# The sample tile's turn behind the first token tile, and a layer norm in parts of 160 and 384 tokens

## The chip, the cores and the metric

The program runs on one core of a Trainium2 chip. The metric is the device time of one execution in microseconds. Before the change it is 1164.78 us, the median of three runs from 1162.54 to 1170.73.

## The reference, cut to what matters

A two-layer decoder trunk is run on 512 prompt tokens and on 32 sample tokens (8 sequences of 4), all in float32, width 1024. Layer 0 mixes tokens with a short convolution and a windowed attention, layer 1 with a Conformer convolution module. Each is followed by a mixture of experts (32 experts, two for each token). What the change touches is the middle of layer 1:

```
def odd_mixer(h, w_pw1, b_pw1, dw_w, dw_b, ln_g, ln_b, w_pw2, b_pw2, conv_buf):
    ...
    c = causal_dwconv(u_ext, dw_w) + dw_b
    c = jax.nn.silu(layer_norm(c, ln_g, ln_b))
    return c @ w_pw2 + b_pw2, u_ext[:, -(C_KERNEL - 1):]
...
        x = x + y
        x = x + hier_moe(rms_norm(x, p['g_ffn'][layer]), ...)
```

The layer norm runs over the 1024 channels of each token. The 1024 x 1024 product behind it is followed by a residual add, an RMS norm and a router (36 logits for each token).

## The kernel before

The 544 tokens lie in five tiles: tiles 0 to 3 hold 128 prompt tokens each, tile 4 the 32 sample tokens. The convolution's output `cT` has channels in the partitions (8 blocks of 128) and tokens along the rows, so the layer norm's sums over channels are matmuls with a matrix of 1/1024.

`LN_PART` cuts the tokens into two parts, which pass through the layer norm one behind the other. Before the change the first part is tokens 256 to 543 (288 columns: tiles 2, 3 and the sample tile), the second tokens 0 to 255 (256 columns: tiles 0 and 1). I call them part A and part B. The steps are:

- DVE subtracts the mean from part A and then from part B, 8 instructions each (L1735).
- ACT squares part A (L1078), POOL squares part B (L826).
- PE sums the squares of A (`variance(0)`, L2359), keeps busy with five matmuls without use (L1796), multiplies the samples' rows with the weights (`project_samples`, L2038), sums the squares of B (`variance(1)`, L2359).
- For each part: ACT takes the root (L1081), DVE its reciprocal (L1739) and scales 8 blocks (L1747), ACT applies silu to them (L1085). ACT has a table to load between root and silu, 1.28 us each time.

Then come the tiles, in the order `ODD_ORDER` (4, 2, 3, 0, 1), on PE in `project`. A tile of 128 tokens is 16 matmuls (L2081), 8 for each half of the output's columns; the trace shows each float32 matmul as two records. For the sample tile `project_samples` does this already. The rest of a tile's work is: ACT moves the samples' sums out of PSUM (L854, the sample tile only), DVE adds bias and residual to X (L1155, L1162), PE turns the tile by eight transposes (`turn`, L1788) into PSUM banks 6 and 7, DVE copies it to SBUF (`keep`, L1168), PE multiplies by the router's weights (`router`, L2101), DVE makes logits and picks experts (`logits`, `pick_...`). A tile's turn stands between the two halves of the next tile's matmuls, its router in the middle of the second half. The sample tile's turn must also wait until the variance of part B has been read from bank 7 (`std_ready`).

The order on each engine is the order in which the code is written; each engine waits at semaphores. `experts(1)` follows: it ranks the tokens by expert, gathers their rows, and runs 32 experts, whose weights come in over the SP queue into six slots (L540, L542 ahead, L599 and L603 as slots come free). A token's rank in its expert goes by tile order (`ODD_ORDER`), in both layers. Tokens beyond an expert's first 64 are worked on in further jobs.

Of the kernel before, what the change touches and what calls it, by code (L numbers as in the profile page):

```python
# [35 lines left out]
TOK = SEQ + SAMPLES  # L36
# [19 lines left out]
PE_CONV = (1, 4, 6, 7)  # L56
DVE_CONV = tuple(c for c in range(KD) if c not in PE_CONV)
PW1_SLOT = (2, 3, 0, 1)
LN_PART = ((256, TOK), (0, 256))
ODD_ORDER = (4, 2, 3, 0, 1)  # L60
PART_AT = (2, 5, 7)
DVE_TAPS = (((0, 1, 17),), ((0, 17, 31),), ((2, 1, 25),), ((2, 25, 31), (3, 1, 10)), ((3, 10, 25),),
            ((3, 25, 31), (5, 1, 19)), ((5, 19, 31),), ())
# [75 lines left out]
def program(nc, x_in, w_mix0, kv_in, w_out, w_pw1, w_pw2, w_moe, smalls, consts, masks, rows, st_a, st_c,  # L139
            y_out, k_out, v_out, ua_p_out, ua_s_out, uc_p_out, uc_s_out):  # L140
    ctx = ExitStack()
    with ctx:
# [272 lines left out]
        def tiles_of(call):  # L415


            return list(enumerate(ODD_ORDER if call % 2 else range(TILES)))

# [675 lines left out]
        def _(dve):  # L1095
# [48 lines left out]
            def norm_and_route(call, done):  # L1144

                n = call // 2
                logits, pick_group, pick_first, pick_second, places = routing(n)

                def update(s, h):
                    i = ODD_ORDER[s]  # L1150
                    r = ROWS[i]
                    cols = slice(512 * h, 512 * h + 512)
                    if call == 3 and h == 0:

                        link(nc.vector.tensor_tensor(X[0:r, i, :], X[0:r, i, :], brow[0:r, :], ALU.add))  # L1155
                    if s == 0:
                        dve.wait_ge(spread_kept, n + 1)
                        src = xn_of(call, s, i)[0:r, cols]
                    else:
                        dve.wait_ge(done, 2 * s + h)  # L1160
                        src = psum[0:r, 2 * (s % 2) + h, :]
                    nc.vector.tensor_tensor(X[0:r, i, cols], X[0:r, i, cols], src, ALU.add).then_inc(x_half, 1)  # L1162

                def keep_half(s, h):
                    i = ODD_ORDER[s]
                    r = ROWS[i]
                    dve.wait_ge(turned, 10 * call + 2 * s + h + 1)
                    nc.vector.tensor_copy(  # L1168
                        turned_tile(s)[:, 4 * h:4 * h + 4, 0:r],
                        psum[:, 6 + h, :].rearrange("p (k t) -> p k t", k=4)[:, :, 0:r]).then_inc(hT_ready, 1)  # L1170

                def keep(s):
                    keep_half(s, 0)
                    keep_half(s, 1)

                def inverse(s):
                    i = ODD_ORDER[s]
                    r = ROWS[i]
                    dve.wait_ge(root_ready, TILES * call + s + 1)
                    nc.vector.reciprocal(stat[0:r, 2, i:i + 1], stat[0:r, 1, i:i + 1]).then_inc(inv_ready, 1)  # L1180

                last = TILES - 1
                update(0, 0)
                update(0, 1)
                for s in range(1, TILES):
                    update(s, 0)
                    keep(s - 1)
                    inverse(s - 1)
                    logits(s - 1)
                    if s == last:  # L1190
                        keep_half(last, 0)
                        pick_group(s - 1)
                    update(s, 1)
                    if s < last:
                        pick_group(s - 1)
                        pick_first(s - 1)
                        pick_second(s - 1)
                pick_first(last - 1)
                keep_half(last, 1)
                inverse(last)  # L1200
                pick_second(last - 1)
                logits(last)
                pick_group(last)
                pick_first(last)
                pick_second(last)
                places()
# [548 lines left out]
            update = combine(1)  # L1755
# [13 lines left out]
        def _(pe):  # L1769
# [292 lines left out]
            def project(call, src, blocks, weights, done, after_first=None):  # L2062
# [3 lines left out]
                for s, i in tiles_of(call):  # L2066
                    r, b = ROWS[i], 2 * (s % 2)
                    if s >= 2:
                        pe.wait_ge(x_half, 10 * n + 2 * (s - 2) + 2)
                    if s == 0 and call == 3:  # L2070
                        project_samples(call, b, src, blocks, weights, done)
                        after_first()
                    for h in range(2 if s else 0):
                        for k in range(blocks):
                            if call == 3 and s == 3 and h == 0:
                                pe.wait_ge(swish_done, KD + k + 1)
                            if h and k == blocks // 2:
                                router(call, s - 1)
                                if s == TILES - 1:
                                    turn(call, s, (0,))  # L2080
                            t = mm(psum[0:r, b + h, :], src[:, k, P * i:P * i + r], weights(k, h),  # L2081
                                   start=k == 0, stop=k == blocks - 1)
                        t.then_inc(done, 1)
                        if h == 0:
                            if s == 1 and call == 3:

                                pe.wait_ge(std_ready, 2)
                            turn(call, s - 1)
                turn(call, TILES - 1, (1,))
                router(call, TILES - 1)  # L2090
# [411 lines left out]
```

## Time and profile before

| what | value |
|---|---|
| median of three runs | 1164.78 us |
| lowest and highest run | 1162.54 and 1170.73 us |
| the profiled execution's own time | 1161.33 us |
| its span, first to last instruction | 1159.6 us |
| PE busy, share of the span | 1030.2 us, 89% |
| DVE, ACT, POOL busy | 427.2, 209.5 and 182.5 us |
| the stretch that the change touches | about 768 to 855 us of the span |

The table gives the size of things only. A busy share is a mean over a dozen stages with different limits, so the stretch around the change has to be read engine by engine in the timeline; times in the rows count from the span's start.

### The profile page before, as it was taken

Reading aid. Unit: us, or ns where it says so; the run is one execution under the profiler, and the core shown is the slowest. Engines: PE = TensorE matmul, PEld = TensorE weight load, DVE = VectorE, ACT = ScalarE, POOL = GpSimd, SP = SyncE. Lnnn points to the kernel's source line nnn. Section 1 sums busy time; section 2 is a strip of 40 time slices with the busy share of each in tenths; the row PEclk is TensorE's granted clock in tenths of the full one; section 3 lists DMA queues with packets and bytes.
Section 4 is the critical chain, followed back from the end, with each engine's and each line's share of the span. In section 5 each row is a group of like instructions: output and inputs, shape, how many; then the busy total and the mean of one; then the engine's idle time right before and its main releaser. Section 6 shows DMA issues by size and latency. Waiting matters only on the chain.

```text
span 1159.6 us, 19198 instructions
## 1 busy us (share of the span) xinstructions
PE 1030.2 (89%) x7043; PEld 654.5 (56%) x7044; DVE 427.2 (37%) x906; ACT 209.5 (18%) x425; POOL 182.5 (16%) x270
## 2 busy tenths in 40 slices
PE   6999998879899987788389989988998999999980
PEld 4887786545655544344167767744566555555540
DVE  3441002454722111111149899635363121111216
ACT  4000102232201110110140101144120111111113
POOL 1000010000042221211103120110004222323120
PEclk9999999989899998898899999999988999999995
DMA  9424023345479999999752010164047999999956
GB/s 359 207 103 160 16 111 75 144 183 219 149 257 409 408 409 409 408 409 412 312 224 73 26 48 1 34 248 186 37 179 230 407 406 402 410 407 397 400 206 233
DMA packets 74512, 281.61 MB, mean 243 GB/s; under 512 B 13182, under 2 KB 13886, under 8 KB 71296
## 3 DMA queue, kind: packets, MB, share of 16 engines
q1 hardware_dynamic: 58192, 253.76, 56.1%
q0 software_dynamic: 11120, 17.89, 4.4%
q10 hardware_dynamic: 5120, 8.87, 2.3%
q8 instruction: 53, 0.87, 0.3%
q14 instruction: 27, 0.22, 0.0%
HBM read 270.75 MB, written 29.65 MB: 259 GB/s over the span
## 4 chain that ended last, share of the span: by engine, by line
PE 63%; DMA 21%; DVE 11%; ACT 2%; issue 2%; SPq 0%; POOLq 0%; DVEq 0%; ACTq 0%; POOL 0%
DMA ring<-w_moe 12%; PE psum L2177 12%; PE psum L2081 7%; DMA ar<-w_moe 6%; PE psum L2244 6%; PE psum L1852 6%; PE psum L2284 5%; PE psum L1808 5%; DVE ar L1711 5%; PE psum L2309 3%; PE psum L1921 2%; PE psum L2160 2%; DVE X L1426 2%; PE psum L2209 1%; PE psum L1796 1%
## 5 line engine op out<-in xcount | busy, mean ns | idle before, releaser
L2177 PE MATMUL psum<-ring,ar 128*64 128x256 f32 x1408 | 175.1, 393 | 18.7 <-DMA ring<-w_moe 16.7
L2177 PEld LDWEIGHTS psum<-ring,ar 128*64 128x64 f32 x1408 | 100.2, 141 | 89.8 <-issue 26.0
L2284 PE MATMUL psum<-ar,ring 128*128 128x272 f32 x512 | 121.3, 398 | 5.3 <-DVE ar L1697 2.9
L2284 PEld LDWEIGHTS psum<-ar,ring 128*128 128x128 f32 x512 | 97.7, 192 | 30.1 <-issue 4.2
L1711 DVE SCALAR_TENSOR_TENSOR ar<-ar,sv 128x512 f32<-128x512 f32 x120 | 107.0, 893 | 5.8 <-ACT ar L1049 1.9
L1634 DVE COPY ar<-psum 128x128 f32<-128x128 f32 x64 | 18.6, 291 | 241.8 <-PE psum L2234 238.3
L2081 PE MATMUL psum<-ring,ar 128*128 128x512 f32 x192 | 90.0, 618 | 4.4 <-DVE ar L1411 4.4
L2177 PE MATMUL psum<-ar 128*64 128x256 f32 x640 | 82.9, 404 | 7.9 <-DMA ar<-w_moe 7.9
L2244 PE MATMUL psum<-ring,ar 128*64 128x512 f32 x352 | 84.1, 599 | 0.8 <-DVE ar L1634 0.8
L2177 PEld LDWEIGHTS psum<-ar 128*64 128x64 f32 x640 | 46.3, 145 | 43.0 <-issue 12.4
L973 ACT ACTIVATE ar<-psum 128x128 f32<-128x128 f32 x64 | 17.7, 277 | 285.9 <-PE psum L2177 285.9
L1808 PE MATMUL psum<-ar,ring 128*128 128x272 f32 x256 | 59.9, 394 | 2.9 <-DVE ar L1137 2.9
L2081 PEld LDWEIGHTS psum<-ring,ar 128*128 128x128 f32 x192 | 36.5, 198 | 45.9 <-issue 45.6
L982 ACT ACTIVATE ar<-psum 128x512 f32<-128x512 f32 x64 | 38.2, 597 | 132.0 <-PE psum L2244 132.0
L1808 PEld LDWEIGHTS psum<-ar,ring 128*128 128x128 f32 x256 | 48.3, 190 | 13.2 <-DVE ar L1137 3.3
L1627 DVE TENSOR_TENSOR ar<-ar,psum 128x128 f32<-128x128 f32 x64 | 18.4, 287 | 99.2 <-ACT ar L973 99.2
L763 POOL DMA_INDIRECT expert_outputs<-ar,ixy x48 | 48.1, 1002 | 41.5 <-POOL ixy L760 41.5
L1616 DVE TENSOR_TENSOR ar<-psum,sv 128x512 f32<-128x512 f32 x64 | 41.2, 686 | 25.3 <-PE psum L2160 25.3
L2244 PEld LDWEIGHTS psum<-ring,ar 128*64 128x64 f32 x352 | 23.3, 136 | 31.8 <-issue 25.1
L1852 PE MATMUL psum<-ar,ring 128*128 128x272 f32 x160 | 38.3, 392 | 0.0
L2244 PE MATMUL psum<-ar 128*64 128x512 f32 x160 | 38.2, 599 | 0.0
L2160 PEld LDWEIGHTS psum<-cst,ar 128*128 128x128 f32 x256 | 31.2, 194 | 12.1 <-issue 11.5
(266 smaller groups left out, 1211.8 us busy)
## 6 DMA issues: line engine op xcount, KB each, us to landing
ring<-w_moe SPq DMA_DIRECT2D x44, 2048.0 KB, 16.6
ring<-w_moe SPq DMA_DIRECT2D x44, 1024.0 KB, 18.6
ar<-w_moe SPq DMA_DIRECT2D x20, 2048.0 KB, 16.4
ar<-w_moe SPq DMA_DIRECT2D x20, 1024.0 KB, 18.4
ring<-w_pw SPq DMA_DIRECT2D x6, 2048.0 KB, 10.8
ring<-w_mix SPq DMA_DIRECT2D x3, 3072.0 KB, 29.9
ring<-expert_outputs SPq DMA_DIRECT2D x6, 1024.0 KB, 9.1
ring<-kv_in SPq DMA_DIRECT2D x2, 2880.0 KB, 11.1
```

The source lines that it names most:

```text
L763: pool.indirect_dma_start(ys_dram, bass.IndirectOffsetOnAxis(index, 0), yj[b], None, bounds_check=4 * TOK - 1, oob_is_err=False).then_inc( ...
L982: nc.scalar.activation(yj[b], psum[:, 4 + u % 2, :], ACT.Copy).then_inc(moe.y_kept, 1)
L1616: nc.vector.tensor_tensor(xt[:, 4 * h:4 * h + 4, :], psum[:, 3 + 4 * h, :].rearrange("p (k t) -> p k t", k=4), bcast(g[:, :, None], [P, 4, ...
L1711: t = nc.vector.scalar_tensor_tensor(out=out, in0=src, scalar=w, in1=out, op0=ALU.mult, op1=ALU.add)
L1808: t = mm(psum[:, proj_bank(m) + h, 0:HALF], w[:, k, :], hT[:, k, HALF * h:HALF * h + HALF], start=k == 0, stop=k == KD - 1)
L1852: t = mm(psum[:, mix_bank(q, what), 0:HALF], w[:, k, :], x[:, k, :], start=k == 0, stop=k == 3)
L2081: t = mm(psum[0:r, b + h, :], src[:, k, P * i:P * i + r], weights(k, h), start=k == 0, stop=k == blocks - 1)
L2160: t = tr(psum[:, 3 + 4 * (k // 4), o:o + P], rows_[:, k, :], ident)
L2177: t = mm(psum[64 * f:64 * f + 64, u % 2, 0:2 * P], xt[:, k, 64 * (u % 2):64 * (u % 2) + 64], w[:, k, f, :], start=k == 0, stop=k == KD - 1)
L2244: t = mm(psum[64 * h:64 * h + 64, 4 + u % 2, :], aT[:, 64 * k:64 * k + 64], slot(u % MSLOTS)[:, o:o + 512], start=k == 0, stop=k == 1)
L2284: t = mm(psum[:, glu_bank(m) + h, 0:HALF], w[:, k, o:o + P], hT2[:, k, HALF * h:HALF * h + HALF], start=k == 0, stop=k == KD - 1)
L2309: t = mm(psum[32 * s:32 * s + 32, 4 + i, :], diags(n)[32 * i:32 * i + 32, j, :], cu[32 * i:32 * i + 32, c, j:j + SEQ], start=j < 4, stop=j ...
```

## The change

The table of parts and the order of tiles are new: part A is tokens 384 to 543 (160 columns: tile 3 and the sample tile), part B tokens 0 to 383 (384 columns: tiles 0, 1 and 2), the tiles go 4, 3, 2, 0, 1. In layer 1 the sample tile's turn stands behind both halves of tile 3 and not between them, its router in the middle of the first half of tile 2 and not of the second half of tile 3. DVE adds both halves of tile 3 to X before it copies the sample tile's turn. The waits for part B's silu move from the fourth tile in order to the third.

```diff
-LN_PART = ((256, TOK), (0, 256))
-ODD_ORDER = (4, 2, 3, 0, 1)
+LN_PART = ((384, TOK), (0, 384))
+ODD_ORDER = (4, 3, 2, 0, 1)
...
                 for s in range(1, TILES):
                     update(s, 0)
-                    keep(s - 1)
-                    inverse(s - 1)
-                    logits(s - 1)
+                    if s == 1 and call == 3:
+
+                        inverse(0)
+                        update(1, 1)
+                        keep(0)
+                        logits(0)
+                    else:
+                        keep(s - 1)
+                        inverse(s - 1)
+                        logits(s - 1)
...
-                    update(s, 1)
+                    if s > 1 or call == 1:
+                        update(s, 1)
...
-                            if call == 3 and s == 3 and h == 0:
+                            if call == 3 and s == 2 and h == 0:
                                 pe.wait_ge(swish_done, KD + k + 1)
+                            if call == 3 and s == 2 and h == 0 and k == blocks // 2:
+                                router(call, 0)
                             if h and k == blocks // 2:
-                                router(call, s - 1)
+                                if call == 1 or s > 1:
+                                    router(call, s - 1)
...
                         t.then_inc(done, 1)
-                        if h == 0:
-                            if s == 1 and call == 3:
-
+                        if s == 1 and call == 3:
+
+                            if h:
                                 pe.wait_ge(std_ready, 2)
+                                turn(call, 0)
+                        elif h == 0:
                             turn(call, s - 1)
```

PE in layer 1, from the first part's variance on, before (L2359 variance, L1796 the matmuls without use, L2038 `project_samples`, L2081 a tile, L1788 turn, L2101 router):

```order
L2359 MATMUL psum<-ar,cst 128x288 x8
L1796 MATMUL psum<-cst 128x384 x5
L2038 MATMUL psum<-ring,ar 32x256 x32
L2359 MATMUL psum<-ar,cst 128x256 x8
L2081 MATMUL psum<-ring,ar 128x512 x8
L1788 MATMUL psum<-cst,X 128x32 x8
L2081 MATMUL psum<-ring,ar 128x512 x4
L2101 MATMUL psum<-sv,ring 32x36 x8
L2081 MATMUL psum<-ring,ar 128x512 x12
L1788 MATMUL psum<-cst,X 128x128 x8
```

The same place after the change (the same code has higher line numbers: 2372, 1804, 2046, 2092, 1796, 2114):

```order
L2372 MATMUL psum<-ar,cst 128x160 x8
L1804 MATMUL psum<-cst 128x384 x5
L2046 MATMUL psum<-ring,ar 32x256 x32
L2372 MATMUL psum<-ar,cst 128x384 x8
L2092 MATMUL psum<-ring,ar 128x512 x16
L1796 MATMUL psum<-cst,X 128x32 x8
L2092 MATMUL psum<-ring,ar 128x512 x4
L2114 MATMUL psum<-sv,ring 32x36 x8
L2092 MATMUL psum<-ring,ar 128x512 x4
L1796 MATMUL psum<-cst,X 128x128 x8
```

Sixteen matmuls of a tile instead of eight stand between the second variance and the sample tile's turn; four and four instead of twelve stand around the sample tile's router.

DVE at the same place, before (L1735 subtracting the mean, L1739 reciprocal, L1747 scaling, L1155 and L1162 additions to X, L1168 the copy of the turned tile):

```order
L1735 TENSOR_TENSOR ar<-ar,psum 128x288 x8
L1735 TENSOR_TENSOR ar<-ar,psum 128x256 x8
L1739 RECIPROCAL ar<-ar 128x288
L1747 TENSOR_TENSOR ar<-ar 128x288 x8
L1739 RECIPROCAL ar<-ar 128x256
L1747 TENSOR_TENSOR ar<-ar 128x256 x8
L1155 TENSOR_TENSOR X<-X,ar 32x1024
L1162 TENSOR_TENSOR X<-X,ring 32x512 x2
L1155 TENSOR_TENSOR X<-X,ar 128x1024
L1162 TENSOR_TENSOR X<-X,psum 128x512
L1168 COPY ring<-psum 128x4x32 x2
L1180 RECIPROCAL stat<-stat 32x1
```

And after:

```order
L1743 TENSOR_TENSOR ar<-ar,psum 128x160 x8
L1743 TENSOR_TENSOR ar<-ar,psum 128x384 x8
L1747 RECIPROCAL ar<-ar 128x160
L1755 TENSOR_TENSOR ar<-ar 128x160 x8
L1747 RECIPROCAL ar<-ar 128x384
L1755 TENSOR_TENSOR ar<-ar 128x384 x8
L1155 TENSOR_TENSOR X<-X,ar 32x1024
L1162 TENSOR_TENSOR X<-X,ring 32x512 x2
L1155 TENSOR_TENSOR X<-X,ar 128x1024
L1162 TENSOR_TENSOR X<-X,psum 128x512
L1180 RECIPROCAL stat<-stat 32x1
L1162 TENSOR_TENSOR X<-X,psum 128x512
```

The copy of the turned sample tile (L1168) comes one row later, behind the addition of tile 3's second half.

POOL's only change is in the squares of part B:

```order
L826 TENSOR_TENSOR ar<-ar 128x256 x8
```

```order
L826 TENSOR_TENSOR ar<-ar 128x384 x8
```

Its eight instructions are half as wide again.

## Rows read from the trace of the kernel before

**Rows 1.** The page: GB/s in 40 slices; the chain that ended last, by engine.

```profile
GB/s 359 207 103 160 16 111 75 144 183 219 149 257 409 408 409 409 408 409 412 312 224 73 26 48 1 34 248 186 37 179 230 407 406 402 410 407 397 400 206 233
...
PE 63%; DMA 21%; DVE 11%; ACT 2%; issue 2%; SPq 0%; POOLq 0%; DVEq 0%; ACTq 0%; POOL 0%
```

**Rows 2.** Timeline of PE, 764 to 850 us: start, us, engine, line, what, [idle before <-releaser].

```profile
768.76 4.15 PE L2359 MATMUL psum<-ar,cst 128*128 128x288 f32 x16 [1.02 <-ACT ar L1078]
772.74 3.39 PE L1796 MATMUL psum<-cst 128*128 128x384 f32 x10
776.91 4.17 PE L2038 MATMUL psum<-ring,ar 128*32 128x256 f32 x64 [0.78 <-ACT ar L1085]
781.02 3.72 PE L2359 MATMUL psum<-ar,cst 128*128 128x256 f32 x16
784.58 7.03 PE L2081 MATMUL psum<-ring,ar 128*128 128x512 f32 x16
795.50 0.94 PE L1788 MATMUL psum<-cst,X 32*128 32x32 f32 x8 [3.90 <-DVE X L1162]
796.37 5.40 PE L2081 MATMUL psum<-ring,ar 128*128 128x512 f32 x8
...
813.62 3.60 PE L2081 MATMUL psum<-ring,ar 128*128 128x512 f32 x8
```

**Rows 3.** Timeline of DVE, 764 to 800 us.

```profile
767.77 5.65 DVE L1735 TENSOR_TENSOR ar<-ar,psum 128x288 f32<-128x288 f32 x16 [15.67 <-PE psum L2327]
773.48 1.95 DVE L1739 RECIPROCAL ar<-ar 128x288 f32<-128x288 f32 x1
775.46 3.23 DVE L1747 TENSOR_TENSOR ar<-ar 128x288 f32<-128x288 f32 x8
785.28 1.75 DVE L1739 RECIPROCAL ar<-ar 128x256 f32<-128x256 f32 x1 [6.60 <-ACT ar L1081]
787.07 2.77 DVE L1747 TENSOR_TENSOR ar<-ar 128x256 f32<-128x256 f32 x8
...
794.67 1.28 DVE L1162 TENSOR_TENSOR X<-X,ring 32x512 f32<-32x512 f32 x2 [3.71 <-ACT ring L854]
```

**Rows 4.** Timeline of ACT, 764 to 800 us.

```profile
768.26 2.99 ACT L1078 ACTIVATE ar<-ar 128x288 f32<-128x288 f32 x8 [1.82 <-DVE ar L1735]
...
776.14 4.25 ACT L1085 ACTIVATE ar<-ar,sv 128x288 f32<-128x288 f32 x8 [1.40 <-DVE ar L1747]
...
784.78 0.47 ACT L1081 ACTIVATE ar<-psum,eps 128x256 f32<-128x256 f32 x1 [3.08 <-PE psum L2359]
...
787.53 4.04 ACT L1085 ACTIVATE ar<-ar,sv 128x256 f32<-128x256 f32 x8 [0.98 <-DVE ar L1747]
```

**Rows 5.** Timeline of POOL, 764 to 900 us.

```profile
771.19 4.61 POOL L826 TENSOR_TENSOR ar<-ar 128x256 f32<-128x256 f32 x8 [20.30 <-DVE ar L1735]
```

**Rows 6.** One line each: durations min/median/max in ns, first and last start.

```profile
L1747 DVE TENSOR_TENSOR ar<-ar x16: 415/433/646, 775.5 to 789.4; 128x288 f32<-128x288 f32 x8, 128x256 f32<-128x256 f32 x8
...
L1711 DVE SCALAR_TENSOR_TENSOR ar<-ar,sv x120: 740/752/2544, 611.6 to 741.4; 128x512 f32<-128x512 f32 x120
...
L820 POOL TENSOR_TENSOR ar<-ar,sv x8: 2162/2581/2610, 612.6 to 748.7; 128x992 f32<-128x992 f32 x8
```

**Rows 7.** Windows: us, busy of each engine (count), PEclk, DMA share, GB/s.

```profile
796.00:800.00 4.00, 3.99 (x9) 1.90 (x10) 2.52 (x7) 2.58 (x4) 0.00 (x0) 0.62 0.88 350
806.75:811.71 4.96, 4.96 (x13) 2.27 (x12) 4.44 (x18) 1.44 (x3) 0.00 (x0) 1.00 0.01 2
```

**Rows 8.** Timeline of PE in layer 0's experts.

```profile
540.10 3.74 PE L2177 MATMUL psum<-ar 128*64 128x256 f32 x20 [2.21 <-DMA ar<-w_moe]
...
556.25 2.38 PE L2177 MATMUL psum<-ring,ar 128*64 128x256 f32 x20 [1.95 <-DMA ring<-w_moe]
```

**Rows 9.** Timeline of the SP queue: the first load into a freed slot, layer 1.

```profile
889.76 0.38 SPq L599 DMA_DIRECT2D ring<-w_moe  x1
```

**Rows 10.** The chain that ended last, 950 to 1160 us.

```profile
963.61 6.74 DMA ar<-normed_rows,ixe
```

## The prediction

> **What bounds the kernel now.** I read the page first: the chain that ended last is PE for 63% and DMA for 21% of the span, and in the last quarter the DMA moves about 405 GB/s slice after slice, which is the experts of layer 1 [rows 1]. So two questions have to be kept apart: what the changed stretch gains, and whether the experts behind it pass the gain on. For the first I read the timelines of PE, DVE, ACT and POOL around the layer norm [rows 2 to 5].
>
> PE is the engine that sets the end of this stretch. It has one large hole: behind the first half of tile 2 (784.58 + 7.03 = 791.6) it wants to turn the sample tile, and stands for 3.90 us until DVE has the samples' sums in X [rows 2, 3]. The chain that it waits for starts with the second variance: root at 784.78, reciprocal 785.28 to 787.03, scaling, silu 787.53 to 791.57, the samples' move out of PSUM, X from 794.67 [rows 3, 4]. The hole has a second price behind it. The eight records after the turn take 5.40 us, where the same eight take 3.60 us later, and the granted clock of 796 to 800 is 0.62, which is a stretch at 1.2 GHz within one at 2.4 [rows 2, 7].
>
> For the second question: the first expert weights that need a freed slot are issued at 889.76 [rows 9], after the routing, and the full DMA rate begins with them (slice 32 of 40) [rows 1]. A slot is freed by PE's work, so this start moves with PE. Before it the DMA has slack (179 and 230 GB/s in slices 30 and 31). I therefore carry a gain of the stretch to the end at its full size.
>
> **Part 1: the turn moved.** Before, 8 matmuls (16 records, 7.03 us) stand between the second variance and the turn; now 16 stand there, 14.06 us. The chain of the samples takes, from the end of the variance (784.74) to the turn's start (795.50), 10.8 us before. After, it is longer by the wider part B, 384 columns for 256:
> - root: 0.47 us, at most 0.24 more; I take 0.1;
> - reciprocal: 1.95 us at 288 columns, 1.75 at 256, so 6.25 ns a column and +0.80 at 384 [rows 3];
> - the first scaling: +0.15 (2.77/8 = 0.35 us at 256, half as much again at most);
> - eight silus: 4.25 us at 288 and 4.04 at 256, so 0.82 ns a column and instruction, +0.84 [rows 4].
>
> That is 10.8 + 1.9 = 12.7 us against 14.06. The turn waits for nothing any more, with 1.4 us to spare. The 3.90 us go, and with them the slow stretch, 5.40 - 3.60 = 1.80. Gain 5.7 us. The order of the matmuls otherwise costs nothing, since the count is the same.
>
> What is late next? In tile 2's first half PE waits for part B's silus: the last ends at about the variance + 8.8, before PE is through with tile 3 at + 14.06. DVE adds tile 3's second half before it copies the turned samples, but that half is done when the turn begins, and the router that wants the copy stands 4 matmuls (3.6 us) behind it, against 0.69 + 0.48 of DVE work. The picks of the samples and the next bias addition (4.96 us, [rows 7]) now stand between the samples' router and tile 2's first addition. With 0.35 for the logits, 0.7 for the addition and 1.28 for the copy, that is 7.3 us to the end of tile 3's copy, while PE needs 3.5 + 0.9 + 3.5 = 7.9 until its router. It fits by 0.6 us; if it does not, some tenths are lost.
>
> **Part 2: the parts of 160 and 384.** DVE subtracts the mean from the same 544 columns, 5.65 us from 767.77, and takes no reciprocal before both parts are through: 773.48 in both kernels [rows 3]. ACT's squares of A and the variance of A end earlier, which gains nothing because of that. The reciprocal of A takes 1.95 - 128 x 0.00625 = 1.15, so scaling can start at 774.65, 0.8 earlier than before. Eight scalings of 160 take about 0.25 each (between 0.22, in proportion, and 0.35, no gain from the width), eight silus 0.53 - 0.10 = 0.43 each. Left alone the samples' product would end at about 779.1 in place of 781.09.
>
> But POOL is still at its squares then. Before it is busy from 771.19 to 775.80 with part B [rows 5]. After, part B is centred from 769.7 on, POOL starts at about 770.25 and needs 8 x 0.576 x 1.5 = 6.9 us, to 777.2. The trace shows what a DVE instruction that reads two tensors from SBUF does beside POOL's products: one of the 512-wide ones took 2544 ns against a median of 752, while POOL's took 2581 against 2162 alone [rows 6]. The first scaling of A, which began at 775.46 while POOL ran to 775.80, took 646 ns against about 444 [rows 3, 5, 6], and 775.80 + 0.30 is just where it ended. So the two take turns, whole instructions at a time. After the change the first scaling waits for POOL's sixth square (to 775.4), the second for the seventh (776.5), the third for the eighth (777.55), and the other five are free: 777.75 + 5 x 0.43 puts the last silu's start at 779.9, its end at 780.4, and the samples' product ends at 780.95. The 0.8 + 1.2 us that narrower instructions offered are gone but for 0.1.
>
> Then the second variance: 16 records, 3.72 us at 256 columns; the part that goes by columns is 3.55, so 5.4 at 384 [rows 2]. It ends at 786.3 against 784.74 before. Cost of part 2: 1.5 us. The squares of POOL end before it begins (777.9 against 780.95), so they are no wait.
>
> The Trainium skill speaks against this change at just this place. Its page "SBUF — State Buffer", section "Who interferes with whom", says that a DVE instruction with two SBUF inputs contends with a GpSimd instruction that reads SBUF, and that the one that comes second is blocked for the whole of the first. By that rule part 2 costs the 1.5 us above; without it part 2 would gain 0.2. The 2544 and 646 ns agree with the rule.
>
> **The sum.** -3.90 - 1.80 + 1.50 = -4.2 us. The profiled execution (1161.33 us, span 1159.6) would come to 1157.1, its span to 1155.4. It lies 3.45 us under the median, and I carry the same difference over: 1164.78 - 4.2 = 1160.6 us. A change of 1%, 11.6 us, is about what a measurement of this kernel can tell from none, so this is "within 1%".
>
> **Rivals.**
> - POOL and DVE do not hinder each other here (the waits seen were of other instructions, mostly 992 wide). Then part 2 gains 0.2: -5.9, 1158.9 us. Against it speaks the 646 ns.
> - PE's clock falls before the samples' product. The matmuls without use end 0.8 + 1.5 us earlier against the silus: the first variance is paced by squares of 160 columns (2.99/8 = 0.37 us each at 288, some 0.28 at 160) and ends at 770.8, so PE stands from 774.1 to 776.1, 2.0 us where it was 0.78, and then works in bursts of 0.45 us with gaps of 0.6. A wait of 2.21 us in layer 0 was followed by 20 records in 3.74 us, one of 1.95 by the same 20 in 2.38 [rows 8]. The price is that of such a stretch, 1.4 to 1.8: -2.5, 1162.3 us. For it: 2.0 with further gaps behind; against: the 1.95 row. The Trainium skill's page "TensorE: Matmul & The Clock Gate", section "HAM oscillation — how this bites in real kernels", has waits between short bursts as the thing that makes the next burst start at the low clock, which would be this case.
> - The gain does not reach the end, because the experts wait for weights: 0, 1164.8 us. Against it: the loads' start moves with PE [rows 9].
> - Slower: the order of the tiles sets which tokens of a crowded expert fall into its further job, in both layers. Such a job's gather stood on the last chain once, 6.74 us at 963.61 [rows 10]. If one more gather comes to stand there, -4.2 + 6.7 = +2.5, 1167.3 us. It decides as soon as PE reaches a further job before its rows are in. Against it: the number of jobs goes by counts, which the order leaves as they are.
> - More than forecast: the routing behind the stretch, or a run of clock changes, falls better by 3 us: -7, 1157.5 us.
>
> **Chances.** The forecast (contention, warm clock) 0.40; no contention 0.15; the clock falls 0.23; nothing reaches the end 0.07; slower by a gather 0.07; more than forecast 0.08. The range must take in the second and third case and the spread of medians of three (the runs before lie 8 us apart, the lower two 2.2): 1155.5 to 1166. All cases lie within 1% but for the tails of the last two: faster by over 1% 0.04, within 0.93, slower 0.03.
>
> **What the profile after would show.** The wait before L1796 (the turn of the samples, 32x32) gone, and the eight records behind it at 3.6 us: part 1 right. Scalings of 128x160 of which three take 0.5 us and more, and POOL's squares near 0.9 to 1.1 us: the contention right; all near 0.3 us, wrong. The start of the second variance near 781 and its length near 5.4. A granted clock below 1.00 between 776 and 782: the second rival. The first load of L599 earlier by the same amount as the stretch: carried to the end. I would be wrong if the turn still waits, which needs a samples' chain 1.4 us longer than worked out, or if the routing after it takes another time at all.

## The result, and the profile after

The changed kernel takes 1160.12 us, the median of 10 runs, against 1167.66 us for the kernel before in 10 runs: a ratio of 0.9942, 95% interval 0.9928 to 0.9956, which is 5.1 to 8.4 us. The first three runs of before, from which the forecast's median was taken, lay low within that kernel's runs. The experiments below were timed in four further groups of runs; the first of these gave 0.996 (0.994 to 0.9979) for the change. A run far above all others of its kernel (1264.39 us among the 10 of before, 4504.34, 1366.08 and 5736.39 us in three of the experiments) counts in the medians but not in the ratios. The profiled execution took 1160.78 us with a span of 1159.0, only 0.6 us under that of before, because it came to the layer norm 3.0 us later: DVE starts to subtract the mean at 770.80, where it started at 767.77 [rows 3]. Ahead of that point the change touches only the order of the tiles in layer 0 and the widths of the mean's matmuls in layer 1 (160 and 384 columns for 288 and 256, 544 in all as before). So I read every trace from this point on, which I call the mean's end.

The timeline of PE after, to be laid beside [rows 2]:

```profile
771.54 4.12 PE L2372 MATMUL psum<-ar,cst 128*128 128x160 f32 x16 [0.78 <-ACT ar L1078]
775.50 3.39 PE L1804 MATMUL psum<-cst 128*128 128x384 f32 x10
778.90 1.41 PE L2046 MATMUL psum<-ring,ar 128*32 128x256 f32 x16
780.55 2.80 PE L2046 MATMUL psum<-ring,ar 128*32 128x256 f32 x48 [0.23 <-ACT ar L1085]
783.27 5.43 PE L2372 MATMUL psum<-ar,cst 128*128 128x384 f32 x16
788.54 13.90 PE L2092 MATMUL psum<-ring,ar 128*128 128x512 f32 x32
802.37 0.68 PE L1796 MATMUL psum<-cst,X 32*128 32x32 f32 x8
802.97 3.70 PE L2092 MATMUL psum<-ring,ar 128*128 128x512 f32 x8
...
815.09 1.87 PE L2114 MATMUL psum<-sv,ring 128*128 128x36 f32 x16
```

The sample tile's turn (802.37) has no wait in front of it, where [rows 2] has 3.90 us, and the eight records behind it take 3.70 us in place of 5.40. The tiles' matmuls start 788.54 - 770.80 = 17.74 us after the mean's end; before 784.58 - 767.77 = 16.81. The second router, from which on both kernels issue the same instructions, starts at 44.29 after the mean's end. Before it was 817.05 - 767.77 = 49.28. The stretch is 4.99 us shorter. (That the instructions behind it are the same does not mean that they take the same time; the table of the experiments shows where they do not.)

DVE after, beside [rows 3]:

```profile
770.80 5.66 DVE L1743 TENSOR_TENSOR ar<-ar,psum 128x160 f32<-128x160 f32 x16 [15.66 <-PE psum L2340]
776.37 1.14 DVE L1747 RECIPROCAL ar<-ar 128x160 f32<-128x160 f32 x1
777.55 3.57 DVE L1755 TENSOR_TENSOR ar<-ar 128x160 f32<-128x160 f32 x8
789.35 2.55 DVE L1747 RECIPROCAL ar<-ar 128x384 f32<-128x384 f32 x1 [8.24 <-ACT ar L1081]
...
800.53 1.28 DVE L1162 TENSOR_TENSOR X<-X,ring 32x512 f32<-32x512 f32 x2 [3.64 <-ACT ring L854]
```

Eight scalings of 160 columns take 3.57 us, more than eight of 288 did (3.23). Of POOL the timeline shows the squares of part B, and the view of the scalings' line from 777.5 to 779.6 us has the first three:

```profile
773.28 6.47 POOL L826 TENSOR_TENSOR ar<-ar 128x384 f32<-128x384 f32 x8 [19.36 <-DVE ar L1743]
```

```profile
L1755 DVE TENSOR_TENSOR ar<-ar x3: 656/943/943, 777.5 to 779.0; 128x160 f32<-128x160 f32 x3
```

Three scalings of 0.66 to 0.94 us while POOL works, and the shortest is 0.311 after it: this is the taking of turns. The chain that ended last runs right through them (start, us, what):

```profile
771.50 4.69 DVE ar L1743 x13
...
776.37 1.16 DVE ar L1747
...
777.55 2.40 DVE ar L1755 x3
...
779.97 0.53 ACT ar L1085
...
780.55 2.80 PE psum L2046 x48
783.34 5.36 PE psum L2372 x16
788.70 13.73 PE psum L2092 x32
```

Windows of the same kernel: the granted clock (the number behind the five engines) is 0.58 around 774, so mostly at 1.2 GHz, and full (2.4) at the place of the old slow stretch of [rows 7].

```profile
772.00:776.00 4.00, 4.00 (x17) 3.87 (x16) 4.00 (x12) 2.69 (x7) 2.72 (x4) 0.58 1.03 421
...
796.00:800.00 4.00, 4.00 (x10) 1.74 (x10) 0.90 (x1) 3.91 (x8) 0.00 (x0) 1.00 1.04 417
```

The first load into a freed slot comes at 887.51, so 116.71 us after the mean's end where it was 121.99 [rows 9]:

```profile
887.51 0.38 SPq L599 DMA_DIRECT2D ring<-w_moe  x1
```

### The profile page after: what moved, and what is told of

It is laid out like the page before. It is cut to its first block, busy times and chain, and to the rows that moved or that the text cites. A ratio compares the mean times of both kernels' runs of the same rounds, so it can differ in the third digit from the quotient of the medians.

```text
span 1159.0 us, 19197 instructions
## 1 busy us (share of the span) xinstructions
PE 1028.3 (89%) x7043; PEld 650.7 (56%) x7044; DVE 429.2 (37%) x906; ACT 208.7 (18%) x425; POOL 184.5 (16%) x270
## 4 chain that ended last, share of the span: by engine, by line
PE 63%; DMA 22%; DVE 12%; issue 2%; ACT 2%; SPq 0%; POOLq 0%; DVEq 0%; ACTq 0%; POOL 0%
DMA ring<-w_moe 13%; PE psum L2190 11%; PE psum L2092 7%; DMA ar<-w_moe 6%; PE psum L1860 6%; PE psum L2257 5%; PE psum L2297 5%; PE psum L1816 5%; DVE ar L1719 5%; PE psum L2322 3%; PE psum L1929 2%; PE psum L2173 2%; PE psum L1804 1%; PE psum L2222 1%; DVE X L1434 1%
## 5 line engine op out<-in xcount | busy, mean ns | idle before, releaser
L2297 PE MATMUL psum<-ar,ring 128*128 128x272 f32 x512 | 122.9, 402 | 5.2 <-DVE ar L1705 3.0
L2190 PE MATMUL psum<-ar 128*64 128x256 f32 x640 | 77.1, 383 | 9.9 <-DMA ar<-w_moe 9.9
L2190 PEld LDWEIGHTS psum<-ar 128*64 128x64 f32 x640 | 43.8, 137 | 42.5 <-issue 12.8
L1816 PE MATMUL psum<-ar,ring 128*128 128x272 f32 x256 | 61.6, 402 | 2.8 <-DVE ar L1137 2.8
L1860 PE MATMUL psum<-ar,ring 128*128 128x272 f32 x160 | 38.3, 392 | 0.0
```

Source lines behind the costliest of these rows:

```text
L1816: t = mm(psum[:, proj_bank(m) + h, 0:HALF], w[:, k, :], hT[:, k, HALF * h:HALF * h + HALF], start=k == 0, stop=k == KD - 1)
L1860: t = mm(psum[:, mix_bank(q, what), 0:HALF], w[:, k, :], x[:, k, :], start=k == 0, stop=k == 3)
L2190: t = mm(psum[64 * f:64 * f + 64, u % 2, 0:2 * P], xt[:, k, 64 * (u % 2):64 * (u % 2) + 64], w[:, k, f, :], start=k == 0, stop=k == KD - 1)
L2297: t = mm(psum[:, glu_bank(m) + h, 0:HALF], w[:, k, o:o + P], hT2[:, k, HALF * h:HALF * h + HALF], start=k == 0, stop=k == KD - 1)
```

## The experiments

The table has what each trace shows, in us after that execution's mean's end: the start of the tiles' matmuls (behind the second variance), the second router, the first load into a freed slot, the end of the span. The column "routing" is the way from the second router to the first matmul of layer 1's experts. The last two columns are the time. The first traces of both kernels are included.

| kernel | tiles | 2nd router | routing | first load | end | median (runs) | ratio, 95% interval |
|---|---|---|---|---|---|---|---|
| before, first trace | 16.81 | 49.28 | 66.22 | 121.99 | 391.83 | | |
| before, again | 16.81 | 49.28 | 63.12 | 120.55 | 392.10 | 1166.18 (12) | 0.9993, 0.9967 to 1.0018 |
| changed, first trace | 17.74 | 44.29 | 66.47 | 116.71 | 388.20 | 1160.12 (10) | 0.9942, 0.9928 to 0.9956 |
| changed, again | 17.74 | 44.29 | 66.44 | 117.34 | 387.09 | 1160.59 (12) | 0.996, 0.994 to 0.9979 |
| turn alone | 18.25 | 44.80 | 66.28 | 117.14 | 390.28 | 1160.4 (12) | 0.9948, 0.9923 to 0.9972 |
| turn alone, again | 18.33 | 44.88 | 66.38 | 116.88 | 388.31 | 1159.44 (6) | 0.9926, 0.9912 to 0.994 |
| parts alone | 17.75 | 52.56 | 63.10 | 122.98 | 394.75 | 1166.06 (12) | 0.9996, 0.9972 to 1.002 |
| parts alone, again | 17.74 | 52.47 | 63.10 | 123.78 | 395.41 | 1167.5 (12) | 1.0, 0.9984 to 1.0016 |
| order alone | 16.81 | 49.28 | 63.12 | 119.41 | 389.20 | 1166.17 (12) | 0.9986, 0.9961 to 1.0011 |
| hole filled | 18.30 | 49.09 | 63.11 | 119.15 | 390.82 | 1163.63 (12) | 0.9972, 0.9954 to 0.999 |
| reciprocal in PSUM | 16.63 | 43.18 | 66.46 | 115.60 | 386.99 | 1159.17 (8) | 0.9918, 0.9888 to 0.9947 |
| variance ahead, 288/256 | 14.75 | 41.40 | 66.33 | 115.23 | 388.02 | 1158.0 (8) | 0.9921, 0.9895 to 0.9946 |
| variance ahead, 160/384 | 13.44 | 40.09 | 65.14 | 111.17 | 380.96 | 1158.04 (7) | 0.9917, 0.9888 to 0.9947 |
| both | 13.30 | 39.95 | 65.10 | 112.54 | 384.45 | 1155.29 (6) | 0.9899, 0.9881 to 0.9916 |

The ratios are against the kernel before in the same group of runs. Their intervals reach 1.6 to 3.4 us to each side; the columns "tiles" and "2nd router" repeat to a tenth of a microsecond as long as the clock does the same. So what is worth a microsecond is read from the stretch, and the time tells whether it arrives.

The routing takes two times. It took 63.1 us in five of the six traces in which the sample tile's turn stands between the halves, and 65.1 to 66.5 us in all eight in which it stands behind both. The difference is the clock, not the work: the same matmuls, in the kernel before run again (granted clock 1.00 from 866 to 872 us) and in the changed kernel (0.50 from 858 to 864 us):

```profile
865.51 1.23 PE L2117 MATMUL psum<-ar,cst 128*128 128x96 f32 x10
...
885.80 3.67 PE L2177 MATMUL psum<-ring,ar 128*64 128x256 f32 x32 [0.95 <-DVE ar L1616]
```

```profile
858.18 2.23 PE L2130 MATMUL psum<-ar,cst 128*128 128x96 f32 x10
...
881.56 3.67 PE L2190 MATMUL psum<-ring,ar 128*64 128x256 f32 x32 [0.94 <-DVE ar L1624]
```

In both, PE had just waited twice, 0.85 and about 0.40 us, with the same matmuls between, so what it did just before does not tell them apart. The first trace of before is the exception among the six: its routing ran at the low clock as well (66.22 us). Why the low clock comes with the moved turn is open.

**The changed kernel again.** No edit.

> The changed kernel once more, as a measure for the others of this group. Forecast theory: ratio 0.9942 as before (about -6.7 us against the kernel before), stretch from the last mean matmul's end to the second router about 5 us shorter. If the 6.7 us were a draw of the chip or of the day, the ratio comes out nearer to 0.9964 (the 4.2 us of the sum).

The stretch is the same to 0.01 us. The ratio, 0.996, lies between those of the two theories (0.9942 and 0.9964), and its interval holds both.

**The kernel before again.** No edit.

> The kernel before against itself: ratio 1.000 within its interval. Its runs spread over 8 us where those of the changed kernel spread over 3; if the spread belongs to the kernel, it shows here again, and the trace of this execution should differ from the first one in some granted clock or wait.

The stretch is that of the first trace to 0.01 us (16.81, 49.28), with the same hole and the same slow records:

```profile
790.21 7.03 PE L2081 MATMUL psum<-ring,ar 128*128 128x512 f32 x16
801.13 0.94 PE L1788 MATMUL psum<-cst,X 32*128 32x32 f32 x8 [3.89 <-DVE X L1162]
802.00 5.40 PE L2081 MATMUL psum<-ring,ar 128*128 128x512 f32 x8
```

But its mean's end is at 773.40, 5.6 us later than in the first trace. The spread lies ahead of the stretch. Its runs go from 1158.9 to 1168.8, those of the changed kernel from 1158.6 to 1164.0. They lie in two clusters: four of the twelve took 1158.9 to 1160.8 us, as short as runs of the changed kernel, and eight 1165.9 to 1168.8.

**The turn alone.** The diff of the change without its two tables, and the wait for silu at `s == 3` as before:

```diff
-LN_PART = ((384, TOK), (0, 384))
-ODD_ORDER = (4, 3, 2, 0, 1)
+LN_PART = ((256, TOK), (0, 256))
+ODD_ORDER = (4, 2, 3, 0, 1)
...
-                            if call == 3 and s == 2 and h == 0:
+                            if call == 3 and s == 3 and h == 0:
                                 pe.wait_ge(swish_done, KD + k + 1)
```

> Only the turn of the sample tile is moved behind both halves of the next tile; parts of 288 and 256 tokens and the order 4, 2, 3, 0, 1 as before. Theory A (the hole behind the first half, 3.9 us, and its slow stretch, 1.8 us, are the whole gain, and the parts cost 1 to 1.5 us): 5.7 us faster than before, about 1 us faster than the changed kernel; ratio about 0.995. Rival B (the parts carry part of the gain): slower than the changed kernel by 1 us or more. In the trace A wants no wait before the turn and the tile's matmuls starting 17 us after the mean's end.

As fast as the changed kernel (1160.4 and 1160.59 us). The hole and the slow records are gone, but the tiles start at 18.25 and not at 16.8, and the trace says why: the first variance took 5.78 us where [rows 2] has 4.15.

```profile
772.51 5.78 PE L2372 MATMUL psum<-ar,cst 128*128 128x288 f32 x16 [1.02 <-ACT ar L1078]
```

**The turn alone, again.**

> The kernel with the turn alone moved, a second time. Its first trace had the first variance at the low clock (5.78 us against 4.15) and its tiles started 18.25 us after the mean. Theory A (with part A at 288 columns the first variance lies on the path, so its clock shows in the end): with a warm variance the tiles start at 16.8 and the second router at 43.4, about 1 us before the changed kernel; with a cold one 18.25 and 44.8 again. Rival: 18.25 whatever the clock.

```profile
772.18 5.84 PE L2372 MATMUL psum<-ar,cst 128*128 128x288 f32 x16 [1.02 <-ACT ar L1078]
...
789.52 13.90 PE L2092 MATMUL psum<-ring,ar 128*128 128x512 f32 x32
```

The low clock again, 18.33. A variance at full clock was not caught in this kernel. The code up to the tiles is that of the kernel before, though, which has 16.81 with a variance of 4.15 in three traces (order alone is the third), so the second router at about 43.4 with a full clock is an inference, not a measurement.

**The parts and the order alone.** The kernel before with the two tables of the change and the wait for silu at `s == 2`; the turn stays between the halves.

```diff
-LN_PART = ((256, TOK), (0, 256))
-ODD_ORDER = (4, 2, 3, 0, 1)
+LN_PART = ((384, TOK), (0, 384))
+ODD_ORDER = (4, 3, 2, 0, 1)
...
-                            if call == 3 and s == 3 and h == 0:
+                            if call == 3 and s == 2 and h == 0:
```

> Only the parts of 160 and 384 tokens and the order 4, 3, 2, 0, 1; the turn stays between the two halves of the first token tile. Theory A: the second part's chain is 1.9 us longer and starts 0.9 us later, so the wait before the turn grows from 3.9 to about 5.8 us, the slow stretch stays: 2 to 3 us slower than before, ratio 1.002. Rival B (the parts carry gain): not slower than before.

```profile
788.80 7.03 PE L2081 MATMUL psum<-ring,ar 128*128 128x512 f32 x16
801.62 1.15 PE L1788 MATMUL psum<-cst,X 32*128 32x32 f32 x8 [5.79 <-DVE X L1162]
802.70 5.64 PE L2081 MATMUL psum<-ring,ar 128*128 128x512 f32 x8
```

The hole is 5.79 us as worked out, the stretch 3.28 us longer than before. The time is not: 1166.06 us.

**The same again.**

> The parts and the order alone, a second time: the first time its stretch was 3.3 us longer than before (second router at 52.56 us after the mean against 49.28), its time not (ratio 0.9996, interval 0.9972 to 1.002). Theory A (the 3.3 us are real in the stretch and were covered by the spread of executions): second router at 52.5 again, ratio 1.000 to 1.005. Rival C (something behind the stretch gives them back in every execution): ratio 0.998 to 1.000 again and a shorter way from the first weight load to the end than before's 272 us.

Stretch 52.47, from the mean's end to the end of the span 395.41 us, 3.3 to 3.6 more than in the two traces of before, and the ratio is 1.0 with an interval that ends at 1.0016, or 1.9 us. From the first load to the end it is 271.6 us, with 269.8 and 271.6 in the traces of before. So rival C's shorter way is not there. The two traces of this kernel show one more thing: the first variance took 2.44 us in the first and 4.12 in the second, and the tiles start at 17.75 and 17.74. By the stretch the kernel should be 3 us slower and by the time it is not. What makes up for it would have to lie ahead of the mean's end, where single traces scatter by 5.6 us; but these two reach it at 771.05 and 770.89 us, between the 767.77 and 773.40 of before. This stays open.

**The order of the tiles alone.** `ODD_ORDER = (4, 3, 2, 0, 1)` in the kernel before.

> The kernel before with only the order of the tiles changed to 4, 3, 2, 0, 1, in both layers. The two kernels with the new order came out 2 to 4 us lower against their stretch than the two with the old one. Theory A (the order does nothing, that difference was the spread of single executions): same as before, ratio 1.000, the number of further jobs and their waits the same. Rival C (the order carries 2 to 4 us through the experts): 2 to 4 us faster, ratio 0.9975, with a shorter expert phase in layer 0 or 1.

Same time as the kernel before run again (1166.17 and 1166.18 us), same stretch. The order does nothing that these runs can tell.

**The hole filled.** The kernel before, with five matmuls without use ahead of the turn:

```diff
                             if s == 1 and call == 3:
-
+                                stay_warm(5, 4)
                                 pe.wait_ge(std_ready, 2)
                             turn(call, s - 1)
```

> The kernel before with five more matmuls without use in the hole ahead of the sample tile's turn (3.2 of its 3.9 us). Theory A (the hole has two prices, the wait itself and a stretch at the low clock behind it): the wait for the turn stays at its end, the eight records behind it go from 5.40 to about 3.6 us, the second router comes 1.8 us earlier; 1.8 us in the whole. Rival: the eight records are slow for the DMA that runs beside them; then 5.4 us stays.

```profile
796.15 3.39 PE L1796 MATMUL psum<-cst 128*128 128x384 f32 x10
800.21 0.94 PE L1788 MATMUL psum<-cst,X 32*128 32x32 f32 x8 [0.67 <-DVE X L1162]
801.08 3.70 PE L2081 MATMUL psum<-ring,ar 128*128 128x512 f32 x8
```

```profile
800.00:804.00 4.00, 3.68 (x15) 2.07 (x16) 3.22 (x9) 2.43 (x4) 0.00 (x0) 1.00 1.02 410
```

The eight records take 3.70 us, although the DMA moves 410 GB/s beside them now (the window's last number; the clock is 1.00). So they were slow for the clock and not for the DMA. From the tiles' start to the second router it is 49.09 - 18.30 = 30.79 us against 32.47: 1.68 us, and the interval of the ratio, 1.2 to 5.4 us, holds it. (The first variance was slow here as well, 5.83 us, hence 18.30, and so the second router itself comes only 0.19 us earlier than before.)

**The reciprocal of part A in PSUM.** The changed kernel, in which DVE reads one of two inputs of the first eight scalings from PSUM:

```diff
-                link(nc.vector.reciprocal(std[:, lo:hi], std[:, lo:hi]))
+                inv = std[:, lo:hi] if h else psum[:, 5, 0:hi - lo]
+                link(nc.vector.reciprocal(inv, std[:, lo:hi]))
...
-                    nc.vector.tensor_tensor(cT[:, k, lo:hi], cT[:, k, lo:hi], std[:, lo:hi], ALU.mult
+                    nc.vector.tensor_tensor(cT[:, k, lo:hi], cT[:, k, lo:hi], inv, ALU.mult
```

> The changed kernel, but part A's reciprocal is written to a free PSUM bank, so DVE's eight scalings of A read one tensor from SBUF and one from PSUM. Theory A (turns taken with POOL's squares): the scalings go from 3.57 us to about 2.1, none is longer than 0.35 us, POOL's squares are a little shorter, the samples' product loses its gap of 0.23 us and ends 0.7 us earlier; in the whole 0.7 us, too little to be seen in the time. Rival D (the scalings are slow for another reason, their width or silu): 3.57 us stays.

```profile
779.57 1.94 DVE L1756 TENSOR_TENSOR ar<-ar,psum 128x160 f32<-128x160 f32 x8
```

```profile
775.29 6.33 POOL L826 TENSOR_TENSOR ar<-ar 128x384 f32<-128x384 f32 x8 [19.36 <-DVE ar L1743]
```

1.94 us for 3.57, at the same widths and with POOL just as busy. The tiles start at 16.63 where they started at 17.74: the contention cost 1.11 us, somewhat more than the 0.7 expected. (The first variance was at full clock here, 2.44 us, and slow in both traces of the changed kernel; that is not the cause, since the parts alone had 17.75 with a variance of 2.44.) PE now stands 1.37 us ahead of the samples' product, waiting for ACT's first silu:

```profile
780.59 3.66 PE L2047 MATMUL psum<-ring,ar 128*32 128x256 f32 x64 [1.37 <-ACT ar L1085]
```

**The second variance ahead of the samples' product.** On the kernel with the turn alone, and then on the changed kernel:

```diff
             variance(0)
-            stay_warm(5, 4)
+            variance(1)
...
-                    lambda: variance(1))
+                    lambda: None)
```

> The kernel with the turn alone moved, and the second part's variance put ahead of the samples' product, in place of the five matmuls without use; its squares are done by then. Theory A (PE is the bound between the product and the tiles): the tiles start 3.6 us earlier, nothing waits at the turn (2.8 us to spare), about 3.5 us faster than the kernel with the turn alone moved, near 1157 us. Rival E (without the matmuls without use PE's clock falls before or in the product, or the samples' chain becomes the bound): 1.5 us or less is left.

```profile
769.86 9.29 PE L2372 MATMUL psum<-ar,cst 128*128 128x288 f32 x32 [1.02 <-ACT ar L1078]
779.52 4.17 PE L2046 MATMUL psum<-ring,ar 128*32 128x256 f32 x64 [0.37 <-ACT ar L1085]
783.63 14.00 PE L2092 MATMUL psum<-ring,ar 128*128 128x512 f32 x32
```

The tiles start at 14.75, 3.5 us before those of the turn alone, as expected. As in both traces of the turn alone the variances began at the low clock (0.58 in the window from 770 to 774); here DVE waited 1.74 us for part A's root because of it. With 0.9921 the time is 9 us under before, where the stretch has 7.9.

> The changed kernel (parts of 160 and 384) with the second variance ahead of the samples' product in the same way. POOL's squares of 384 columns end 9 us after the mean, so the variance and the product behind it wait for them: product from 9.1 to about 13.5 us after the mean. Theory A: tiles start at 13.5 us instead of 17.7, about 4 us faster than the changed kernel, level with the 288 and 256 version. Rival: the wait for POOL's squares lets the clock fall and costs 1.5 to 2 us of it.

```profile
770.38 2.44 PE L2372 MATMUL psum<-ar,cst 128*128 128x160 f32 x16 [0.78 <-ACT ar L1078]
773.00 6.56 PE L2372 MATMUL psum<-ar,cst 128*128 128x384 f32 x16 [0.17 <-POOL ar L826]
779.49 3.66 PE L2046 MATMUL psum<-ring,ar 128*32 128x256 f32 x64
783.08 14.00 PE L2092 MATMUL psum<-ring,ar 128*128 128x512 f32 x32
```

The tiles start at 13.44, 4.3 us before the changed kernel's, as expected. The product has no wait, since it stands behind the variance anyway. In the time these gains are not shown one by one: the intervals of both versions overlap with those of the kernels that they were made from.

**Both together.**

> The changed kernel with the second variance ahead of the samples' product and part A's reciprocal in PSUM. The contention on DVE is gone, but the product then stands behind the second variance, which waits for POOL's squares. Theory A: POOL's squares take 6.33 instead of 6.47 us, so the tiles start 13.3 us after the mean where they started at 13.44: no difference from the version without the PSUM bank (1158 us). Rival: the waits on DVE still set the pace there, and another 1.1 us goes.

```profile
775.71 1.94 DVE L1756 TENSOR_TENSOR ar<-ar,psum 128x160 f32<-128x160 f32 x8
```

In the stretch it is 0.14 us, as expected: the contention is gone and nothing had waited for it. The median of six is 1155.29 us, the lowest of all, ratio 0.9899. The intervals of this and of the version with DVE's scalings from SBUF overlap, so that the PSUM bank helps here is not shown. That this kernel is faster than the kernel before (9.8 to 13.9 us) is; against the changed kernel its stretch is 4.3 us shorter, and its interval does not touch either of that kernel's.

## Why the prediction was right, point by point

**The hole and its slow stretch: right.** The forecast had 3.90 + 1.80 = 5.7 us. From the tiles' start to the second router it is 26.55 us after and 32.47 before: 5.92. (The turn itself also went from 0.94 to 0.68 us.) The hole filled with useless work parts the two: 1.68 us are the clock's. The turn alone has the whole gain of the change in its time.

**Nothing waits at the new turn: right.** DVE begins to add the samples at 800.53, PE comes to the turn at 802.37. The forecast's spare 1.4 us were 1.0: before, the turn began 0.83 us after that addition (794.67 to 795.50), so it could have begun at 801.36. From the end of the second variance that is a samples' chain of 12.7 us, as forecast; the 16 matmuls took 13.9 and not 14.06. The picks of the samples ahead of tile 2's addition cost nothing either: second router without a wait.

**The parts: right in sign, too large by 0.6 us.** Forecast 1.5, measured 17.74 - 16.81 = 0.93. All of the difference is in the contention: without it the forecast had a gain of 0.2, and the changed kernel with the reciprocal in PSUM has one (16.81 - 16.63 = 0.18); for the contention it had 1.7, and that kernel shows 1.11. The terms one by one: POOL starts 2.48 us after the mean's end, as worked out; its squares take 6.47 us in all, 0.82 to 0.91 each, where the forecast had 6.9 without the waits and 0.9 to 1.1 each; the three blocked scalings are there, the first 0.66 and the others 0.94 us, but the third ends 9.2 us after the mean's end and not 10.0; the samples' product ends 12.5 us after the mean's end, forecast 13.2; the second variance takes 5.43, forecast 5.4. So the cost of POOL's squares at 384 columns is the term that was sized too large. The 0.93 also holds only where the first variance of before ran at full clock. Where it was slow, 288 columns started the tiles at 18.25 to 18.33, and against that the parts of the change gain 0.5.

The Trainium skill's page "SBUF — State Buffer", section "Who interferes with whom", agrees with the trace on both sides: it has a DVE instruction with two SBUF inputs blocked by one of GpSimd that reads SBUF, and one with at most one SBUF input free of it. The blocked DVE instruction took 943 ns against 311. With one input from PSUM, beside the same squares, eight took 1.94 us, so none of them was blocked.

**The gain arrives at the end: right in the number, wrong in the account.** Counted from the mean's end, the first load comes 3.2 to 5.3 us earlier and the end 3.6 to 5.0 us, between the two traces of either kernel. The time says 5.1 to 8.4 in one group and 2.5 to 7.0 in the other. But the prediction carried the gain over at its full size, put nothing for the routing, and named it as a sign of being wrong "if the routing after it takes another time at all". It does: 66.5 us, where the kernel before took 66.2 in its first trace and 63.1 in its second. From the second router to the end the eight traces with the moved turn take 343.9 us on average (340.9 to 346.6) and the six others 342.0 (339.9 to 342.9), so some 2 us of the 4.99 seem to be given back there; with such a scatter that is an indication and no more. The 4.2 us of the sum thus fit the 3.6 to 5.0 at the end in part by luck, since the stretch gained 0.8 more than forecast and the routing behind it took longer.

The time, in its turn, shows more than the traces. In the ratio the gain is larger than forecast by 1 to 4 us in the first group, and the first three runs of before, low as they were, made the forecast of 1160.6 us look better than its 4.2 us were. The turn alone and the versions behind it also come out 0.5 to 4 us better in time than in the stretch, the hole filled 3 and the parts alone 3 to 4. A cause that acts on all of them would have to lie outside the stretch. An earlier mean's end is not what the traces show: it lies at 770.4 us on average in the six with the old turn and at 770.5 in the eight with the new one. What they do show is that the two shortest profiled executions with the old turn (1161.33 and 1159.19 us) have it at 767.8 and 768.2 and the other four, at 1163.5 us and more, at 770.9 to 773.4; so how many such short runs a median takes in can move it by some us. This stays open.

**The rivals.** No contention: wrong, by the three scalings. The low clock before the product: wrong. The granted clock is 1.00 from 776 to 782 in the changed kernel. In its two traces the wait did not come up, because the first variance was slow and the matmuls without use ran right up to the product. It did come up in the parts alone, 1.70 us where the forecast had 2.0, and the clock stayed at 1.00 there too (776 to 782) and the product was no slower:

```profile
779.17 1.41 PE L2038 MATMUL psum<-ring,ar 128*32 128x256 f32 x16 [1.70 <-ACT ar L1085]
```

What I had not seen is that the clock falls 4 us earlier, in the first variance, which took 4.12 us in both traces of the changed kernel and 2.44 at full clock (with the reciprocal in PSUM). It cost nothing there (the two traces of the parts alone, 17.75 us without it and 17.74 with it, show that), since DVE is busy with both subtractions until 776.46 and takes no reciprocal before. The same fall costs 1.5 us in the kernels with 288 columns in part A. This is what the narrow part is good for. Nothing reaches the end: wrong, by the 3.6 to 5.0 us there. The routing falls better by 3 us: the opposite was seen, as said above. The gather: the same single one stands on the chain after, as long as in [rows 10]:

```profile
961.31 6.75 DMA ar<-normed_rows,ixe
```

## What to carry to other kernels

A wait of the engine that sets the end has a second price if its clock falls in it; here 3.9 us of waiting cost 5.6 to 5.9. Before matmuls without use are put into such a gap, look whether real work that is already ready stands behind it, as the second variance did: moved ahead it gave 3.5 to 4.3 us in the stretch, nearly as much again as the change. And when work is moved to a slower engine's side or made wider there, look which instructions of its neighbour overlap with it: three short DVE instructions on the path took two to three times as long, and moving one input to PSUM gave that back. Last, code behind a change need not take the time that it took, though it is the same code: the routing here took 2.0 to 3.4 us more than in most traces with the old turn.

## What the runs showed of the hardware that was not expected

The same gap leads to a low clock in one execution and not in the next. In the parts alone the first variance stood behind a wait of 0.78 us in both traces and took 2.44 us in one and 4.12 in the other. In front of layer 1's first products, a wait of 1.94 us was followed by 16 records in 3.94 us in one trace of the kernel before, and one of 1.88 us by the same 16 in 5.62 us in the other:

```profile
596.19 5.62 PE L2284 MATMUL psum<-ar,ring 128*128 128x272 f32 x16 [1.88 <-DVE ar L1137]
```

Such falls, some in each execution, make up a good part of the 5.6 us by which two traces of one kernel reach the same point at different times: this one and another like it at 17 us of the span (3.94 and 5.56 us for 16 records) cost 1.7 and 1.6 us. In the layer norm the first variance ran at 1.2 GHz, wholly or for the most part, in 7 of the 14 traces, always behind the same waits of 0.8 to 1.0 us. In the routing the low clock came in 9 of 14, among them all eight with the moved turn, and cost 2.0 to 3.4 us. A single trace therefore says little about a kernel's time to within 5 us, while a stretch between two fixed points of it repeats to 0.1 as long as its clock is the same in both.
